# A three-block transformer kernel: x loaded ahead of the constants, and the low rank weights fetched five pieces later

## The reference

```python
h = rms_norm(x, norm1_w, 1e-6); z = h @ w_in            # block 1: 2048 -> 8192
y_ssm  = s5_mixer(z[:, :1024], ...)                     # a complex diagonal scan over time
y_attn = diff_attention(q, k, v, ..., rel_table)        # 8 heads, differential softmax
m = sigmoid(gs) * (y_ssm @ w_proj_ssm) + sigmoid(ga) * (y_attn @ w_proj_attn)
x = x + m @ w_out
x = x + (silu(h2 @ w_gate) * (h2 @ w_up)) @ w_down      # h2 = rms_norm(x, norm2_w)
for l in range(2):                                      # blocks 2 and 3
    u = x @ w_in_2[l]                                   # 2048 -> 6080, split in ten parts
    mix = concat(short_conv(...), mla(...), rwkv7(...))
    x = layer_norm(4 ** 0.25 * x + mix @ w_out_2[l])
```

## Time and profile before

| what | us |
|---|---|
| median of 3 runs | 2536.97 (2535.94 to 2538.11) |
| the profiled execution's own time | 2535.61 |
| its span (first to last instruction) | 2533.8 |
| TensorE busy | 2462.4 (97%) |
| VectorE busy | 1475.3 (58%) |
| ScalarE busy | 1128.6 (45%) |
| mean granted TensorE clock | 0.992 of full |
| DMA | 412.43 MB, mean 163 GB/s |

### The profile page before, as it was taken

One profiled execution on the slowest core, in us unless ns is written; L12 is line 12 of the kernel. 1 busy time (PEld: TensorE's weight loads), 2 busy tenths in 40 slices (PEclk: granted clock), 3 DMA queues, 4 the chain that ended last, 5 costly groups with the idle time before them and its releaser, 6 DMA issues.

```text
span 2533.8 us, 45207 instructions
## 1 busy us (share of the span) xinstructions
PE 2462.4 (97%) x19625; PEld 2251.5 (89%) x19625; DVE 1475.3 (58%) x1814; ACT 1128.6 (45%) x1562; POOL 186.0 (7%) x198
## 2 busy tenths in 40 slices
PE   7999999999999999999999999999999999999997
PEld 7777888999889999999988889899888898999885
DVE  4899955565445545445444445745645568456555
ACT  4565555544444444444444434433544535334442
POOL 4000000001000000000000001310100051201000
PEclk9999999999999999999999999999999999999998
DMA  8444444454545665565555566423537664235464
GB/s 233 133 146 149 150 141 132 131 183 164 197 150 183 183 184 182 184 184 183 186 190 191 191 203 181 119 85 110 166 109 232 174 213 141 87 101 150 126 199 166
DMA packets 259126, 412.43 MB, mean 163 GB/s; under 512 B 52912, under 2 KB 73776, under 8 KB 258416
## 3 DMA queue, kind: packets, MB, share of 16 engines
q1 hardware_dynamic: 254496, 395.64, 50.5%
q0 software_dynamic: 4400, 13.89, 2.0%
q10 hardware_dynamic: 32, 0.01, 0.0%
HBM read 403.17 MB, written 6.30 MB: 162 GB/s over the span
## 4 chain that ended last, share of the span: by engine, by line
PE 89%; DVE 6%; ACT 2%; issue 1%; DMA 1%; POOL 0%; SPq 0%; ACTq 0%; DVEq 0%
PE bank L560 88%; DVE wp_lo L1068 2%; ACT wp_hi L1721 1%; DMA xt<-x 0%; PE bank L767 0%; DMA raw<-w_in 0%; DVE r_a L1547 0%; DVE rsd L1193 0%; DVE nsd L1460 0%; DVE r_kb L1549 0%; ACT L1721 0%; DVE xr L1714 0%; DVE xr L1712 0%; SPq L516 0%; DVE sqr L1203 0%
## 5 line engine op out<-in xcount | busy, mean ns | idle before, releaser
L1068 DVE TENSOR_TENSOR wp_lo<-raw,wp_hi 128x1024 fp32r<-128x1024 f32 x740 | 921.0, 1251 | 901.9 <-ACT wp_hi L1721 901.0
L1721 ACT ACTIVATE wp_hi<-raw 128x1024 fp32r<-128x1024 f32 x740 | 782.2, 1060 | 1131.9 <-PE bank L560 1087.1
L560 PE MATMUL bank<-XX_hi,wp_hi 128*128 128x256 f32 x3840 | 1114.5, 290 | 15.5 <-DVE wp_lo L1068 14.3
L560 PE MATMUL bank<-XX_lo,wp_hi 128*128 128x256 f32 x3840 | 1089.0, 284 | 0.0
L560 PE MATMUL bank<-XX_hi,wp_lo 128*128 128x256 f32 x3840 | 1088.6, 283 | 0.0
L560 PEld LDWEIGHTS bank<-XX_hi,wp_hi 128*128 128x128 f32 x3840 | 737.9, 192 | 34.4 <-issue 16.8
L560 PEld LDWEIGHTS bank<-XX_lo,wp_hi 128*128 128x128 f32 x3840 | 738.4, 192 | 2.2 <-issue 1.9
L560 PEld LDWEIGHTS bank<-XX_hi,wp_lo 128*128 128x128 f32 x3840 | 738.0, 192 | 0.0
L560 PE MATMUL bank<-wp_hi,FF_hi 128*128 128x512 f32 x352 | 137.3, 390 | 0.0
L560 PE MATMUL bank<-wp_hi,FF_lo 128*128 128x512 f32 x352 | 137.1, 390 | 0.0
L560 PE MATMUL bank<-wp_lo,FF_hi 128*128 128x512 f32 x352 | 137.1, 389 | 0.0
(11 more groups left out here) (476 smaller groups left out, 2772.7 us busy)
## 6 DMA issues: line engine op xcount, KB each, us to landing
raw<-w_in SPq DMA_DIRECT2D x304, 512.0 KB, 3.8
raw<-w_out SPq DMA_DIRECT2D x96, 512.0 KB, 4.4
raw<-w_ffn_gate SPq DMA_DIRECT2D x88, 512.0 KB, 3.6
raw<-w_ffn_up SPq DMA_DIRECT2D x88, 512.0 KB, 4.4
raw<-w_ffn_down SPq DMA_DIRECT2D x88, 512.0 KB, 3.6
raw<-w_proj_attn SPq DMA_DIRECT2D x16, 512.0 KB, 3.7
raw<-w_proj_ssm SPq DMA_DIRECT2D x16, 512.0 KB, 3.6
raw<-w_glu SPq DMA_DIRECT2D x8, 512.0 KB, 3.4
```

The lines of the kernel that those rows point to most:

```text
L560: return e.matmul(o, lhsT, rhs, start=start, stop=stop, skip_group_check=True)
L1068: return tt(d, src, hi, SUB)
L1721: return e.activation(o, x, func, bias=bias, scale=scale)
```

## The change

SP issues x first. The constants come in three parts: ident (64 KB) and the 11 columns (5.5 KB) as two DMAs on ScalarE's queue ahead of norm1_w, and the middle (flip to reset, 576 KB) on SP's queue behind pieces 0 to 3 and ahead of the S5 loads. `s_ones` is now complete at 32, and `s_s5` counts one DMA more. POOL waits for `s_ones` before it reads two of the columns. The fetch of w2 and a2, with its wait for TensorE, moves from the fourth piece of misc0 (and misc1) to the first piece of the next job, `rk`.

```diff
+COLS_AT = 128 * 4 + 3 * T
+NFIRST = COLS_AT + len(COLS)
 @blk.sync
-        e.dma_start(cst[:, 0:NFIRST], A["consts"][:, 0:NFIRST]).then_inc(s_ones, 16)
         for h in range(2):
             for t in range(2):
                 ... # x
         for p in range(4):
             weights(p)
+        e.dma_start(cst[:, 128:COLS_AT], A["consts"][:, 128:COLS_AT]).then_inc(s_s5, 16)
...
-                if p == OF[name].over + 3:
+                if p == OF[name].over + 8:
                     e.wait_ge(*over(name))
                     e.dma_start(w2a2[0:64, :], A["rwkv_w2_2"][l]).then_inc(s_lora, 16)
                     e.dma_start(w2a2[64:128, :], A["rwkv_a2_2"][l]).then_inc(s_lora, 16)
...
 @blk.tensor, @blk.vector, @blk.scalar
-        e.wait_ge(s_ones, 16)
+        e.wait_ge(s_ones, 32)
-        e.wait_ge(s_s5, 16 * 7)
+        e.wait_ge(s_s5, 16 * 8)
 @blk.scalar
+        for a, b in ((0, 128), (COLS_AT, NFIRST)):
+            e.dma_start(cst[:, a:b], A["consts"][:, a:b]).then_inc(s_ones, 16)
         e.dma_start(first_row[0:16, :], ...)
 @blk.gpsimd
         at.limit("gs2")
+        e.wait_ge(s_ones, 32)
         e.wait_ge(s_c5, 16 * 4)
```

More of the change, by code:

```diff
@@ L33 @@
 COLS = ["eps6", "eps5", "epsg", "halfpi", "sgn", "nsgn", "par0", "par1", "half0", "half1", "freq"]
-NFIRST = 128 * 4 + 3 * T + len(COLS)
+COLS_AT = 128 * 4 + 3 * T
+NFIRST = COLS_AT + len(COLS)
 NCONST = NFIRST + 128 * (len(MATS) - 4)
```

## The result

| kernel | median us | ratio to the kernel before, 95% interval |
|---|---|---|
| before | 2536.45 (6 runs) | |
| changed | 2526.72 (6 runs) | 0.9962 (0.9952 to 0.9972) |

The change takes 9.7 us off; forecast were 8.25 us, 2528.7, in a range from 2526.8 to 2532.4. The median lies 0.1 us under the range's lower edge; by the ratio, 0.9962 of the 2536.97 us on which the forecast was built is 2527.3 us, inside it. The profiled execution took 2526.77 us with a span of 2525.0; the spans differ by 8.8 us.

What follows compares the result with a forecast made beforehand. TensorE, busy 97% of the span, bounds the kernel, so only its idle or slow-clock stretches pay. 6.35 us at misc0 plus 1.9 us at the start, 8.25 us off 2536.97, gave 2528.7 us, range 2526.8 to 2532.4.

Steps and rivals of the forecast that it cites:

- The wait at misc0: Between blocks 1 and 2: without SP's 6.0 us wait, TensorE's 4.80 us gap and 1.55 us of slow clock go.
- What would be late next: At misc0, pieces 6 and 7 meet the store of x but land in time, 1.5 to 2.6 us to spare.
- Rival C: The stall at misc0 moves to piece 6 or 7, colliding with the store of x; 2532.7 us, chance 0.08.
- The start: With x first, its halves land at 6.5 and 10.1 and TensorE's turnings start 1.9 us sooner.
- rival B: The start gives nothing: piece 4 or 6 is caught up with, or the clock comes later; 2530.6 us, chance 0.12.
- Pieces 4 and 6 at their old time: Near the start, their fetches come when they did, rounded at 28.70 and 36.49; spare 3 and 1.5 us, cost zero.
- Zero at misc1: Moving the fetch of w2 and a2 there gains zero, since TensorE waits in the layer norm; at most a few tenths.
- The sum: Whole kernel: 6.35 us at misc0 plus 1.9 us at the start, 8.25 us saved, giving 2528.7 us.

Runs made afterwards that it cites:

- experiment 2: The kernel before with the fetch of w2 and a2 moved five pieces later at misc0 only; 2528.95 us, ratio 0.9969.
- experiment 5: The changed kernel run again, unaltered, beside the kernel before; 2527.78 us, ratio 0.9962.
- experiment 1: The changed kernel with the fetch of w2 and a2 back in its old place, only x first kept; 2533.78 us, ratio 0.9990.
- experiment 3: The kernel before with the fetch of w2 and a2 moved five pieces later at misc1 only; 2537.01 us, ratio 1.0001.
- Experiment 4: The kernel before, SP's wait kept, with POOL storing x (2 MB) only after TensorE is through with misc0; 2528.60 us, ratio 0.9968.
- experiment 6: The changed kernel with the fetch of w2 and a2 one piece later than in the kernel before, instead of five; 2530.42 us, ratio 0.9977.
- experiment 8: The changed kernel with the constants ident to reset (640 KB) all on ScalarE's queue beside x; 2528.19 us, ratio 0.9967.
- experiment 7: The changed kernel with a semaphore for each of x's four DMAs, so ACT squares each quarter as it lands; 2525.37 us, ratio 0.9954.

## Why the prediction held, step by step

**The wait at misc0** (forecast 6.35 us: 4.80 of gap, 1.55 of slow clock). Measured steps of 6.37 us in the changed kernel's profile and 6.38 us in those of experiments 2 and 5. The size is right because gap and slow stretch were taken from the same rows. The medians say 7.75 us in experiment 2; in the profiles of experiments 1 and 3, where the stall stands, it is 0.45 and 0.31 us dearer than in the one I had read, so part of the difference may be an execution of before that had the stall cheap. The mechanism was told rightly but with the weights wrong: I called SP's wait what delays and the store something that pieces 6 and 7 would meet. Experiment 4 shows that without the store the old place costs nothing. For the gain this made no difference, since taking away either of the two causes removes the whole stall; for what else one could have changed it does.

**What would be late next.** I gave pieces 6 and 7 a spare of 2.6 and 1.5 us. Piece 6 could be rounded at 1487.17, wanted at 1490.1 - 1.2 = 1488.9 (the kernel is 1.2 us ahead there): 1.7 us. Piece 7 at 1489.09, wanted at 1491.8: 2.7 us. For rk's first piece I claimed 3 us; in the second profile of the changed kernel it came at 1494.73 after a wait of 3.60 us, and was wanted near 1496.0: 1.3 us. Rival C was not far off.

**The start** (forecast 1.9 us, 6.5 and 10.1 for x's halves). Measured 7.10 and 10.09, TensorE 1.94 us earlier. The 0.01 us at the second half is luck. In the four profiles with x loaded as in the changed kernel (the two of it, experiments 1 and 6) it lands between 9.99 and 10.40, and the first half came 0.60 us later than I said. The price itself holds: those four start their turnings at 14.08 us on average, the four with the constants first (before, experiments 2, 3 and 4) at 16.00, 1.9 us apart. Experiment 8 gives much the same with the bytes on the other queue: 576 KB are 2.0 us at my rate, and cost 1.80. (1024 KB in 3.58 us are 286 KB per us and not 293; the terms of my sum go by the quotients and don't change.)

But not all of it arrived. By piece 22 the profile had 1.12 us left, and at fd3 1.17. Neither piece 4 nor piece 6 held it up: TensorE has no wait for either. The losses are at two places. The 24 turnings took 5.49 instead of 5.20 us, and TensorE came out of an idle stretch of 3.74 us in the S5 branch at the lower clock. The first matmul there in before and in the changed kernel:

```profile
77.40 0.30 PE L699 MATMUL bank<-cst,BP 128*128 128x128 f32 x1 [3.74 <-issue]
```

```profile
75.82 0.45 PE L700 MATMUL bank<-cst,BP 128*128 128x128 f32 x1 [3.74 <-issue]
```

The granted clock over 74 to 78 us is 1.00 in the one and 0.52 in the other. For the turnings the clock is an inference from their pace, 0.21 us each at first and 0.13 later: the granted clock reads 1.00 there in every profile. The Trainium skill (TensorE: Matmul & The Clock Gate, Part 1: The HAM clock gate) warns that the point of release differs between runs, and I had put that into the range. The runs agree: the 24 turnings took 5.49 us in one execution of the changed kernel and 4.34 us in the other. Of rival B's two mechanisms it is the clock that showed, and it took about 0.8 of the 1.95 us. In experiment 1 the lead of 1.87 us was whole up to fd3.

**Pieces 4 and 6 at their old time**: wrong by 1.7 and 1.3 us in the changed kernel (26.98 and 35.17), by 0.6 and 0.3 us in experiment 1 (28.08 and 36.83). The fetches behind `sb` scatter by more than a microsecond.

**Zero at misc1**: right as to the edit (experiment 3), and yet 1.3 of the 8.8 us in the profile lie there. Had I compared only the two traces I should have put them down to the edit. As a forecast of what the whole change does at that place the zero may be wrong all the same: every one of the eight profiles with a lead has the step.

**The sum.** 8.25 us against 9.7 between medians: the forecast was 1.5 us too small. Two terms look short. The stall at misc0 cost 6.38, 6.83 and 6.69 us in the three profiles that have it (before, experiments 1 and 3), 6.6 on average, where I took 6.35. And misc1 stood at zero. Add up for each kernel what the profiles say without misc1: 1.9 us for x first (3.0 in experiment 7, 0.1 in experiment 8), and 6.6 us where the stall is gone (2.9 in experiment 6). The medians of the changed kernel and of experiments 1, 2, 4, 6, 7 and 8 all lie above this, by 0.9 to 1.5 us; each of their profiles has the step of 1.3 us at misc1. Experiment 3, which has no such step, lies 0.3 us under it. That fits a gain at misc1 that comes with any lead, but it isn't shown: the changed kernel in experiment 5 has the step in its profile and its median lies 0.2 us under the sum, experiments of one job share one median of before, each interval reaches 2 us and more to either side, and a median over many runs has no trace. So how the 1.5 us divide stays open.

## What to carry to other kernels

A wait on a queue that prefetches eats reserve, and whether it stalls the consumer was decided here by what else was on the DMA engines just then; either the wait or the large store could be moved, and each was worth the whole. To price it, list the fetches in order with the time at which each buffer comes free, the landing that the trace shows for that place in the queue, and the time at which it is wanted: this found the gap's size, and in experiment 6 its new place. When two traces are compared, make the table of leads first, and hold each step against kernels that lack the edit before it is put down to it. A step that those show too isn't thereby chance: look for what they have in common.

## What the runs showed of the chip that I had not expected

TensorE's clock after a wait isn't a constant of the kernel. The same 24 turnings at the start took 4.34 to 5.49 us over ten profiles; the same 24 matmuls of misc1's first piece took 4.5 us from first to last start in before (2000.06 to 2004.56) and 2.8 us in the changed kernel (1992.85 to 1995.67); a stretch of the attention ran at a granted clock of 1.00 in the changed kernel's first profile, and at 0.66 in its second, which lost 3.1 us there. Each such place is worth 1 to 3 us, as much as the smaller half of this change, and 23 executions of the kernel before spread over 4.5 us (2533.80 to 2538.30).

A transfer on the second queue took its bytes out of the first one's time: with 576 KB beside x, x's second half landed at 11.89 instead of 10.09 us.
